# A hybrid mixer and mixture-of-experts layer: expert token lists made in DRAM, down products one item later

## The chip, the cores and the metric

The kernel runs on one core of one Trainium2 chip. Its time is the device time of one launch, in microseconds (us), and the median of three runs is 2895.78 us (2894.49 to 2897.89). All arithmetic of size is float32 on TensorE (PE). The other engines are VectorE (DVE), ScalarE (ACT), GpSimd (POOL) and SyncE (SP); SP issues nearly all plain DMAs, POOL the indirect ones.

## What is computed

One decoder layer over 1024 tokens of width 1024. Its first 60% (projections, three token mixers, gates) is untouched here. The rest is the output projection with the residual, a normalisation, and this mixture of experts:

```python
scores = sigmoid(h @ router_w)                    # 1024 x 64
# the best 4 of 8 groups, then the best 8 experts of each token; wts: their scores, normed, x 2.5
for e in 64 experts:                              # rt: the tokens that chose e
    hid = silu(h[rt] @ w1[e]) * (h[rt] @ w3[e])   # 1024 -> 256
    y[rt] += (hid @ w2[e]) * wts[rt, e]           # 256 -> 1024
y += (silu(h @ ws1) * (h @ ws3)) @ ws2            # the shared expert
x = x + g2 * y
```

## The kernel before

The 1024 tokens are eight tiles of 128. The routing stage is a loop over the tiles (PE's loop stands behind `shared_down`). For tile i PE does `out_proj(i)` (32 products of 128x512), `route(i-1)` (the normalised rows turned, then the router), and for tile i-2 the shared expert (`shared_up`, 16 products; `shared_down`, two transposes and 8 products) and `rank` (how many tokens before this one chose each expert). DVE does `residual`, `shared_hidden`, `choose` (the top-k), `slots` and `shared_out`. The rows h go to DRAM (`h2_d`, L439) and the residual with the shared expert to `y_d` (`store_shared`, L435), to which the experts' rows are added later by indirect DMAs.

The expert stage is a loop over items. An item is one expert and up to 256 of its tokens; an expert with more gets a further item behind the 64. There are 67 items here. They come in four sizes, which this text calls A (up to 64 tokens), B (65 to 128), C (129 to 192) and D (193 to 256). C and D have a second block of rows: 93 blocks in all, of which 63 are full and 30 are half ones, for which PE packs two 64-row products side by side (`up_half`, `down_half`). For item i (`pe_item`), PE does in this order: the up products of the first block (L1096 full, L1100 half); for C and D the transposes of the second block's rows (L1090), of the first hidden block (L1106) and the second up products; `turn_rows` for the next item (L1090, 8 transposes); the last hidden block's transposes (L1106 full, L1110 half); `token_lists` (L1084), which makes the list of item i+3 as 16 small products of one-hot matrices (`oh`, built by DVE at L1996 and L2000) with the table of token numbers and weights; and the down products (L1115 full, L1122 half). ACT copies turned rows and turned hidden blocks out of PSUM (L1467, L1473) and does the silu (L1470). DVE multiplies the hidden block (L2029), sums the list and makes the indices (L2022, L2026), weighs the outputs (L2033, or L2037 and L2039), and builds the one-hots for item i+4. POOL gathers rows of h (`fetch_first`, `fetch_second`, L608) for the items i+3 and i+2, waits until the earlier scatter has landed (`added.wait(e_sc)`), and scatters the weighed rows with an add into `y_d` (L612).

SP loads an item's three weight blocks of 1024 KB (L429, L430, L431) into one of four buffers once the item four before is done. The first two items' weights are asked for as soon as the last output projection is through. Each engine's order is written out by hand, with semaphores between the engines.

Between the two stages all token lists need the counts of all tiles: DVE writes the token columns and the item table, splits the table into three bfloat16 parts (L2049 to L2052), and three rounds of one-hot, list products and sum give the first three lists, one after the other.

Of the kernel before, what the change touches and what calls it, by code (L numbers as in the profile page):

```python
# [25 lines left out]
P = 128  # L26
# [8 lines left out]
def layer_kernel(nc, a, out):  # L35
# [23 lines left out]
    with ctx:  # L59
# [10 lines left out]
        y_d = dram("y_d", [T + P, D])  # L70

# [33 lines left out]
        def view(at, *shape):  # L105
# [6 lines left out]
            if len(shape) == 3:  # L112
# [50 lines left out]
        slotn = view(0, T)  # L163
# [12 lines left out]
        NX = NE + 4  # L176
        NI = NE + NE // 2
        selall = view(8192, NT, NE)
        posm = view(8704, NT, NX)
        tw = view(9248, NT, NX, 2)  # L180

# [5 lines left out]

        twb = view(5120, 3 * NT * NX).bitcast(BF16).rearrange("p (i e s z) -> p i e s z", e=NX, s=3, z=2)
        rest = view(6912, NT, NX, 2)
        xg = [[view(12288, D), view(13312, D)], [view(7168, D), view(9248, D)]]  # L190
        xgT = [view(14336 + 1024 * j, KD, P) for j in range(2)]
        oh = [view(16384 + 512 * j, T // 2).bitcast(BF16).rearrange("p (i n) -> p i n", n=P) for j in range(2)]
# [6 lines left out]
        lst = sb("lst", [P, 4, 2, 2])  # L199
        tab = sb("tab", [P, 3, NI + 8], I32)  # L200
        NV = NI + 8 - NE
        past, over, items = view(12000, NV)[0:NE, :], view(12040, 3)[0:NE, :], view(12048, 3, NV)[0:NE]
# [70 lines left out]
        e_w = [sem(f"e_w{b}") for b in range(2)]  # L273
        e_clear, e_go = sem("e_clear"), sem("e_go")
        s_tc, s_tp, s_ts, s_tv, s_to = (sem("s_t" + n) for n in "cpsvo")
# [5 lines left out]
        e_oh, e_lst, e_red, e_idx, e_oh1, e_lst1, e_idx1, e_sc, e_all, f_o = (  # L281
            sem("e_" + n) for n in ("oh", "lst", "red", "idx", "oh1", "lst1", "idx1", "sc", "all", "out"))
        e_w += [sem(f"e_w{b}") for b in (2, 3)]
        to_clear = [*e_xg[0], *e_xg[1], *e_Ta, *e_Tb, *e_xTa, *e_xTb, *e_H, *e_si, *e_hid, *e_hT, *e_hc, *e_O, *e_ob,
                    e_oh, e_lst, e_red, e_idx, e_oh1, e_lst1, e_idx1, e_sc, e_all, f_o, *e_w[2:]]
# [68 lines left out]
        def first_slot(eng, i):  # L354
            return eng.value_load(tab[0:1, 2, bass.ds(i, 1)], min_val=0, max_val=T - WIDE)

        I1 = NE - 4
        NC = T // P
# [4 lines left out]
        def _(sp):  # L363
# [63 lines left out]
            def load_expert(e, b):  # L427
# [3 lines left out]
                sp.dma_start(w2[b], one(a["exp_w2"]).rearrange("(k p) n -> p k n", p=P)).then_inc(e_w[b], 16)  # L431
# [11 lines left out]
            for b in range(2):  # L443
                load_expert(b, b)
            for i in range(NT - 3, NT):
                store_shared(i)
            sp.wait_ge(e_clear, 1)
            sp.wait_ge(s_sO, NT)
            sp.wait_ge(e_xg[0][0], 16)
            for b in range(2, 4):  # L450
                load_expert(b, b)
            with sp.Fori(1, I1 // 4) as it:
                for q in range(4):
                    sp.wait_ge(e_oh, 4 * it + q - 1)
                    load_expert(4 * it + q, q)
            with sp.Fori(I1 // 4, NI // 4) as it:
                with sp.If(tokens(sp, 4 * it) > 0):
                    for q in range(4):
                        with sp.If(tokens(sp, 4 * it + q) > 0):
                            sp.wait_ge(e_oh, 4 * it + q - 1)  # L460
                            load_expert(expert_of(sp, 4 * it + q, NE - 1), q)
# [10 lines left out]
        def _(pool):  # L472
# [104 lines left out]
            for n in range(48):  # L577
# [5 lines left out]
                g.dma_start(gt[n % 3], proj_d[row]).then_inc(s_g[n % 3], 16)  # L583
            pool.wait_ge(s_mg, 32)
# [7 lines left out]

# [8 lines left out]
            g.dma_start(y_d[T:T + P, :], xg[0][0]).then_inc(e_sc, 16)  # L602
            pool.wait_ge(s_so[0], 16 * (NT // 2))
# [27 lines left out]
            second, added = Count(pool, "second"), Count(pool, "added", 16, 16)  # L631
            for e in range(2):
                pool.wait_ge(e_idx1, e + 1)
                pool.sem_inc(e_go, 1)
                n = tokens(pool, e)
                fetch_first(n, e, e)
                fetch_second(n, e, e)
            pool.wait_ge(e_idx1, 3)
# [6 lines left out]
            def pool_item(it, q):  # L645
                i, p = 4 * it + q, q % 2
                n, n_2, n_3 = tokens(pool, i), tokens(pool, i + 2), tokens(pool, i + 3)
                now = pool.snap(i + 3)
# [4 lines left out]
                pool.wait_ge(e_ob[0], now)  # L653
# [19 lines left out]

            with pool.Fori(0, I1 // 4) as it:
                for q in range(4):
                    pool_item(it, q)
            with pool.Fori(I1 // 4, NI // 4) as it:
                with pool.If(tokens(pool, 4 * it) > 0):
                    for q in range(4):
                        with pool.If(tokens(pool, 4 * it + q) > 0):  # L680
                            pool_item(it, q)
# [7 lines left out]
        def _(pe):  # L689
# [316 lines left out]
            def route(i):  # L1006
                pe.wait_ge(s_h2, i + 1)
                if i >= 2:
                    pe.wait_ge(s_ya, i - 1)
# [49 lines left out]
            for i in range(NT + 2):  # L1059
                if i < NT:  # L1060
                    out_proj(i)
                if i >= 2:
                    shared_up(i - 2)
                if 1 <= i <= NT:
                    route(i - 1)
                if i >= 2:
                    shared_down(i - 2)
                    rank(i - 2)
# [5 lines left out]
            mm.then_inc(s_cn, 1)  # L1074
            pe.wait_ge(s_tp, 1)
            t.matmul(psum[0:NE, 7, 128:129], strict[0:NE, 0:NE], over[:, 0:1], start=True, stop=True).then_inc(s_ts, 1)
            pe.wait_ge(s_tv, 1)
# [1057 lines left out]
```

## Time and profile before

| | |
|---|---|
| median of 3 runs | 2895.78 us |
| the profiled execution | 2897.56 us, its span 2895.9 us |
| PE busy | 2730.2 us, 94% of the span |
| DVE, ACT, POOL busy | 39%, 20%, 12% |
| mean granted TensorE clock | 0.974 of 2.4 GHz |
| DMA | 442.26 MB, 153 GB/s over the span |
| routing stage, from the first output projection | 1525 to 1787 us |
| gap between the stages | 1787 to 1820 us |
| expert stage on PE | 1820 to 2868 us |

The shares are averages over stages with different limits. The expert stage and the gap ahead of it are 37% of the span, and the change touches these and the routing stage alone. A group's row gives the engine time of its instructions and the idle time of that engine just before them; a matmul's end is modelled, so what one costs in a dense stream is read as the distance between starts.

### The profile page before, as it was taken

Reading aid. Unit: us, or ns where it says so; the run is one execution under the profiler, and the core shown is the slowest. Engines: PE = TensorE matmul, PEld = TensorE weight load, DVE = VectorE, ACT = ScalarE, POOL = GpSimd, SP = SyncE. Lnnn points to the kernel's source line nnn. Section 1 sums busy time; section 2 is a strip of 40 time slices with the busy share of each in tenths; the row PEclk is TensorE's granted clock in tenths of the full one; section 3 lists DMA queues with packets and bytes.
Section 4 is the critical chain, followed back from the end, with each engine's and each line's share of the span. In section 5 each row is a group of like instructions: output and inputs, shape, how many; then the busy total and the mean of one; then the engine's idle time right before and its main releaser. Section 6 shows DMA issues by size and latency. Waiting matters only on the chain.

```text
span 2895.9 us, 32644 instructions
## 1 busy us (share of the span) xinstructions
PE 2730.2 (94%) x10465; PEld 1414.7 (49%) x10466; DVE 1141.2 (39%) x2772; ACT 584.0 (20%) x1037; POOL 343.9 (12%) x344
## 2 busy tenths in 40 slices
PE   5999999999999899999998997999999999999995
PEld 2444555555545355555444444444545545545543
DVE  3374333333246446554345656322223223323222
ACT  3211222222221222331111111111111111111110
POOL 0000000000110000000110000212222222222221
PEclk8999999999999999999999998999999999999998
DMA  7112323321432332222332103877779879979974
GB/s 271 30 29 84 87 73 95 99 90 51 137 81 62 87 80 73 77 88 80 106 114 86 44 37 131 284 229 228 254 223 307 283 245 312 321 227 338 326 243 94
DMA packets 125537, 442.26 MB, mean 153 GB/s; under 512 B 16252, under 2 KB 18404, under 8 KB 108224
## 3 DMA queue, kind: packets, MB, share of 16 engines
q1 hardware_dynamic: 86688, 311.10, 29.8%
q0 software_dynamic: 38752, 129.89, 17.9%
q8 instruction: 58, 0.95, 0.1%
q14 instruction: 39, 0.32, 0.0%
HBM read 371.95 MB, written 81.31 MB: 157 GB/s over the span
## 4 chain that ended last, share of the span: by engine, by line
PE 84%; DVE 6%; issue 5%; ACT 2%; SPq 1%; DMA 1%; DVEq 1%; POOL 0%; POOLq 0%; ACTq 0%
PE psum L740 27%; PE psum L1096 15%; PE psum L1115 8%; PE psum L981 6%; PE psum L1002 4%; PE psum L1100 3%; PE psum L1084 3%; PE psum L938 2%; PE psum L1122 2%; PE psum L833 2%; PE psum L815 2%; PE psum L1055 1%; PE psum L1090 1%; PE psum L824 1%; DVE work L2029 1%
## 5 line engine op out<-in xcount | busy, mean ns | idle before, releaser
L740 PE MATMUL psum<-hT,ring 128*128 128x512 f32 x1152 | 514.1, 599 | 9.5 <-ACT work L1302 8.8
L740 PE MATMUL psum<-ring,hT 128*128 128x512 f32 x896 | 402.7, 604 | 3.0 <-DVE hT L1596 3.0
L740 PEld LDWEIGHTS psum<-hT,ring 128*128 128x128 f32 x1152 | 215.5, 192 | 253.5 <-issue 242.2
L740 PEld LDWEIGHTS psum<-ring,hT 128*128 128x128 f32 x896 | 169.6, 194 | 199.3 <-issue 198.8
L1096 PE MATMUL psum<-hT,work 128*128 128x512 f32 x560 | 249.1, 598 | 0.0
L1470 ACT ACTIVATE work<-psum 128x256 f32<-128x256 f32 x93 | 35.7, 384 | 870.1 <-PE psum L1096 690.8
L1302 ACT ACTIVATE work<-psum 128x512 f32<-128x512 f32 x128 | 76.0, 595 | 636.3 <-PE psum L740 636.1
L2029 DVE TENSOR_TENSOR work<-work,psum 128x256 f32<-128x256 f32 x93 | 39.2, 422 | 403.5 <-ACT work L1470 399.2
L1096 PE MATMUL psum<-ring,work 128*128 128x512 f32 x448 | 197.9, 595 | 0.0
L612 POOL DMA_INDIRECT y_d<-work,put x93 | 148.7, 1599 | 246.9 <-issue 223.8
L608 POOL DMA_INDIRECT work<-h_d,idx x96 | 98.4, 1025 | 629.7 <-DVE idx L2026 373.7
L1096 PEld LDWEIGHTS psum<-hT,work 128*128 128x128 f32 x560 | 105.3, 191 | 134.9 <-issue 134.9
L981 PE MATMUL psum<-work,ring 128*128 128x512 f32 x384 | 165.0, 593 | 0.0
L2033 DVE SCALAR_TENSOR_TENSOR work<-psum,lst,work 128x1024 f32<-128x1024 f32 x63 | 80.9, 1284 | 182.1 <-PE psum L1115 182.1
L1096 PEld LDWEIGHTS psum<-ring,work 128*128 128x128 f32 x448 | 84.1, 190 | 107.6 <-issue 107.6
L1676 DVE CUSTOM_DVE_ANT_0 work<-psum,work 128x128 f32<-128x128 f32 (+6 forms) x56 | 38.7, 692 | 232.0 <-issue 218.4
L1115 PE MATMUL psum<-ring,work 128*128 128x512 f32 x280 | 126.6, 600 | 0.0
L1002 PE MATMUL psum<-ring,hT 128*128 128x512 f32 x256 | 114.5, 607 | 3.5 <-DVE work L1892 2.7
L981 PEld LDWEIGHTS psum<-work,ring 128*128 128x128 f32 x384 | 73.0, 190 | 91.3 <-issue 91.2
L1467 ACT ACTIVATE work<-psum 128x512 f32<-128x512 f32 x188 | 102.1, 595 | 45.5 <-PE psum L1090 42.2
L1084 PE MATMUL psum<-work 128*128 (+1 forms) x1120 | 87.9, 171 | 23.1 <-DVE work L1996 12.1
L1090 PEld LDWEIGHTS psum<-ident,work 128*128 128x128 f32 x752 | 86.2, 141 | 45.5 <-issue 45.5
(353 smaller groups left out, 3209.0 us busy)
## 6 DMA issues: line engine op xcount, KB each, us to landing
ring<-in_exp_w SPq DMA_DIRECT2D x100, 1024.0 KB, 10.9
hT<-in_exp_w SPq DMA_DIRECT2D x68, 1024.0 KB, 9.6
work<-in_exp_w SPq DMA_DIRECT2D x33, 1024.0 KB, 12.9
ring<-in_w_in SPq DMA_DIRECT2D x16, 2048.0 KB, 13.0
proj_d<-work SPq DMA_DIRECT2D x104, 256.0 KB, 2.0
work<-in_ada_w POOLq DMA_DIRECT2D x16, 1024.0 KB, 5.9
work<-proj_d POOLq DMA_DIRECT2D x56, 256.0 KB, 2.9
work<-proj_d POOLq DMA_DIRECT2D x20, 512.0 KB, 5.0
```

Of the source, the lines that this page charges most:

```text
L608: return g.indirect_dma_start(x[0:n], None, h2_d, bass.IndirectOffsetOnAxis(ap=i[0:n], axis=0), bounds_check=T - 1, oob_is_err=False)
L612: return g.indirect_dma_start(y_d, bass.IndirectOffsetOnAxis(ap=i[0:n], axis=0), x[0:n], None, bounds_check=T + P - 1, oob_is_err=True, co ...
L740: mm = t.matmul(bank(u % 3), l, r, start=(k == 0), stop=(k == KD - 1))
L981: mm = t.matmul(bank(n % 3), w[:, k, j * P:(j + 1) * P], yT[br][:, k, half * BW:(half + 1) * BW], start=(k == 0), stop=(k == 3))
L1002: mm = t.matmul(bank(half), hT[:, k, i * P:(i + 1) * P], slot(("wo", half))[:, k, :], start=(k == 0), stop=(k == KD - 1))
L1084: mm = t.matmul(psum[:, 2, 8 * j:8 * j + 6], oh[j][:, i, :], twb[:, i, bass.ds(e, 1), :, :].rearrange("p o s z -> p (o s z)"), start=(i == ...
L1090: mm = t.transpose(psum[:, k // 4, (k % 4) * P:(k % 4 + 1) * P], x[:, k * P:(k + 1) * P], ident[:, :])
L1096: return t.matmul(bank(3 + j), xgT[j][:, k, :], w13[b][:, :, k, :], start=(k == 0), stop=(k == KD - 1))
L1100: mm = t.matmul(psum[HALF * f:HALF * (f + 1), 3 + j, :].rearrange("p (w n) -> p w n", w=2)[:, :, 0:P], xgT[j][:, k, 0:HALF], w13[b][:, :, ...
L1115: mm = t.matmul(bank((6, 0)[j] + half), hidT[j][:, k * P:(k + 1) * P], w2[b][:, k, half * BW:(half + 1) * BW], start=(k == 0), stop=(k == ...
L1467: s.activation(xgT[j][:, 4 * half:4 * half + 4, :].rearrange("p k n -> p (k n)"), bank(half), ACT.Copy).then_inc((e_xTa, e_xTb)[half][j], 1)
L2033: v.scalar_tensor_tensor(out=ob[j][p], in0=banks(b, 2), scalar=lst[:, q, j, 1:2], in1=g2b, op0=ALU.mult, op1=ALU.mult).then_inc(e_ob[j], 1)
```

## The change

1. Routing also makes the lists. `choose` gives each token its eight experts' numbers in order (`cnt`, `eq8`) and their weights, `slots` computes for each of the eight a row of a DRAM table `list_d` (place in the expert's list, then expert), and POOL scatters them: eight indirect DMAs of 128 rows of 8 bytes (token, weight) per tile, 64 in all (`list_tokens`). The table is filled with padding first. Behind the last tile POOL reads the whole table back into SBUF (`lists`, 512 KB), and its first 64 places once more into the other half of the partitions (`lists2`). A list is then two columns of SBUF.
2. `token_lists`, the one-hots, the bfloat16 split and the sums are gone. DVE copies three small slices per item instead (`take_list`).
3. In the expert loop PE does the down products of item i-1 (`downs`) behind the first up products and the row transposes of item i. DVE weighs and POOL scatters one item later too, and POOL's gathers wait for PE's `e_Tb` as well. The few items behind the 64 keep item order (`pe_item_alone`).
4. The up weights have a semaphore of their own, apart from the down weights; those of item i are asked for when the up products of item i-4 are through, the down weights later.
5. In the routing stage the shared expert and its store lag three tiles, not two, `rank` comes right behind `out_proj`, `slots` moves into `residual`. The counting and the item table are laid between the last shared blocks. SP asks for the weights of items 0 and 1 behind the store of tile 4, for those of item 2 when the last shared block is done, and issues the store of tile 7 behind these.

```diff
+            def list_tokens(i):
+                pool.wait_ge(s_dst, i + 1)
+                if i == 0:
+                    pool.wait_ge(s_ls, 16)
+                for k in range(TOPK):
+                    g.indirect_dma_start(list_d, bass.IndirectOffsetOnAxis(ap=dest[:, i, k:k + 1], axis=0), pay[:, i, k, :], None,
+                                         bounds_check=P * NE * NT - 1, oob_is_err=True).then_inc(s_ls, 16)
...
+            list_tokens(6)
+            list_tokens(7)
+            pool.wait_ge(s_ls, 16 + 16 * NT * TOPK)
+            rows = list_d.rearrange("(p r) c -> p r c", p=P)
+            g.dma_start(lists, rows).then_inc(s_ls, 16)
...
+            store_shared(NT - 2)
+            sp.wait_ge(s_sO, NT)
             sp.wait_ge(e_clear, 1)
-            sp.wait_ge(s_sO, NT)
-            sp.wait_ge(e_xg[0][0], 16)
+            load_up(2, 2)
+            load_down(2, 2)
+            store_shared(NT - 1)
+            load_up(3, 3)
...
+                    i = 4 * it + q
+                    sp.wait_ge(e_Tb[0], i - 2)
+                    load_up(i, q)
+                    sp.wait_ge(e_hT[0], i - 2)
+                    load_down(i - 1, (q + 3) % 4)
...
+                    fetch_ahead(it, q)
+                    with pool.If(pool.snap(n_last) > 0):
+                        add_rows(pool.snap(n_last), 1 - q % 2, pool.snap(4 * it + q + 2))
...
+            for i in range(NT + 1):
                 if i < NT:
                     out_proj(i)
                 if i >= 2:
+                    rank(i - 2)
+                if i >= 3:
+                    shared_up(i - 3)
+                if i >= 1:
+                    route(i - 1)
+                if i >= 3:
+                    shared_down(i - 3)
+            shared_up(NT - 2)
+            rank(NT - 1)
...
-                pe.wait_ge(e_oh, now)
-                pe.wait_ge(e_idx, now)
-                token_lists(listed).then_inc(e_lst, 1)
...
+                up_first(it, q, n)
+                pe.reg_mov(n_now, tokens(pe, 4 * it + q + 1))
                 with pe.If(n > P):
+                    turn_second(p)
+                with pe.Else():
+                    turn_next(it, q)
+                with pe.If(pe.snap(n_last) > 0):
+                    downs(pe.snap(n_last), (q + 3) % 4, 16 * (it + 1) if q else 16 * it, pe.snap(4 * it + q + 1))
+                pe.nop()
+                pe.reg_mov(n_last, n)
+                with pe.If(n > HALF):
                     pe.wait_ge(e_hid[0], now)
                     turn_hidden(0)
+                    with pe.If(n > P):
+                        up_second(q, n)
+                        turn_next(it, q)
+                        turn_hidden_second(n)
...
+                link(v.tensor_tensor_scan(out=cnt, data0=ones[:, 0:NE], data1=picked, initial=0.0, op0=ALU.mult, op1=ALU.add))
+                link(v.tensor_tensor(cnt, cnt, picked, ALU.mult))
+                link(v.tensor_tensor(eq8, wide(cnt), col_i[:, 1:TOPK + 1].unsqueeze(2).to_broadcast([P, TOPK, NE]), ALU.is_equal))
+                link(v.tensor_tensor(of8, eq8, wide(sel), ALU.mult))
+                link(v.tensor_reduce(flat8, of8, AX.X, ALU.add))
...
+                link(v.tensor_tensor(of8, eq8, at8.unsqueeze(1).to_broadcast([P, TOPK, NE]), ALU.mult))
+                link(v.tensor_reduce(sum8, of8, AX.X, ALU.add))
...
+            table()
+            dve.wait_ge(s_ls, 16 + 16 * NT * TOPK + 16)
...
+            shared_out(NT - 1)
```

## Rows read from the trace of the kernel before

**Rows 1.** Stretches: busy time of PE, PEld, DVE, ACT, POOL, clock, DMA share, GB/s.

```profile
1742.00:1820.00 78.00, 50.09 (x258) 30.66 (x257) 49.82 (x157) 13.04 (x19) 4.72 (x5) 0.82 0.37 137
1820.00:2870.00 1050.00, 1033.36 (x4684) 531.07 (x4684) 302.57 (x508) 163.18 (x373) 243.40 (x186) 1.00 0.81 265
2418.00:2490.00 72.00, 71.50 (x411) 39.74 (x411) 26.68 (x48) 12.22 (x28) 19.41 (x15) 1.00 1.01 360
```

**Rows 2.** Groups, 1820 to 2870 us: count, busy us, mean ns, idle before.

```profile
L608 POOL DMA_INDIRECT work<-h_d,idx x94 | 96.1, 1023 | 564.2 <-DVE idx L2026 373.7 <-issue 190.5
L1084 PE MATMUL psum<-work 128*128 x1072 | 86.2, 171 | 7.6 <-issue 5.6
...
L2080 DVE COPY put<-idx 128x2 int32<-128x2 int32 x67 | 10.9, 163 | 0.0
L1110 PE MATMUL psum<-ident,work 128*128 128x128 f32 x30 | 9.8, 326 | 2.5 <-DVE work L2029 2.5
```

**Rows 3.** PE's timeline of a B item: start, length, then the instructions.

```profile
1939.30 0.44 PE L1106 MATMUL psum<-ident,work 128*128 128x128 f32 x2
1939.76 1.30 PE L1084 MATMUL psum<-work 128*128 x16
1940.97 3.67 PE L1115 MATMUL psum<-work 128*128 128x512 f32 x8
```

**Rows 4.** The same at the end of a D, an A and a C item.

```profile
1897.37 0.44 PE L1106 MATMUL psum<-ident,work 128*128 128x128 f32 x2
1898.15 1.28 PE L1084 MATMUL psum<-work 128*128 x16 [0.34 <-issue]
1899.35 7.11 PE L1115 MATMUL psum<-ring,work 128*128 128x512 f32 x16
...
2452.49 1.28 PE L1084 MATMUL psum<-work 128*128 x16
2453.81 1.94 PE L1122 MATMUL psum<-work 128*64 128x512 f32 x8
...
2715.27 0.33 PE L1110 MATMUL psum<-ident,work 128*128 128x128 f32 x1
2715.73 1.27 PE L1084 MATMUL psum<-work 128*128 x16
2716.90 3.67 PE L1115 MATMUL psum<-ring,work 128*128 128x512 f32 x8
```

**Rows 5.** POOL's timeline: scatters of a B item (first), then of A items.

```profile
2450.48 1.58 POOL L612 DMA_INDIRECT y_d<-work,put  x1 [3.82 <-DMA y_d<-work,put]
...
2462.26 1.46 POOL L612 DMA_INDIRECT y_d<-work,put  x1 [5.98 <-issue]
...
2651.17 1.44 POOL L612 DMA_INDIRECT y_d<-work,put  x1 [5.85 <-issue]
...
2660.52 1.56 POOL L612 DMA_INDIRECT y_d<-work,put  x1 [3.32 <-issue]
```

**Rows 6.** Issue to landing: of L435's stores, of L431's down weights, of L612's scatters.

```profile
DMA to landing us min/median/max: 2.6/3.7/12.4
...
DMA to landing us min/median/max: 10.4/12.9/24.6
...
DMA to landing us min/median/max: 4.8/8.3/12.8
```

**Rows 7.** The chain that ended last: start, length, instructions, around the stages' border.

```profile
1687.73 6.26 PE psum L1055 x8
...
1726.89 13.80 PE psum L1002 x32
...
1752.75 3.70 PE psum L1055 x8
...
1819.87 8.45 PE psum L1096 x16
```

**Rows 8.** A DVE operation over 512 columns: busy us, mean ns.

```profile
L1941 DVE TENSOR_TENSOR work<-work 128x512 f32<-128x512 f32 x6 | 4.2, 692 | 0.2
```

More of the change, by code:

```diff
@@ new lines, in turn_second, with turn_next, turn_hidden_second @@
+            def turn_second(p):
+                fetched[p].up()
+                fetched[p].wait(e_xg[1][p])
+                turn_rows(1, xg[1][p])
+            def turn_next(it, q):
+                pe.wait_ge(e_xg[0][1 - q % 2], 32 * it + 16 * ((q + 1) // 2) + 16)
+                turn_rows(0, xg[0][1 - q % 2])
+            def turn_hidden_second(n):
+                with pe.If(n > P + HALF):
+                    second.wait(e_hid[1])
+                    turn_hidden(1)
+                with pe.Else():
+                    second.wait(e_hid[1])
+                    turn_half_hidden(1)
+                pe.nop()
@@ new lines, in downs @@
+            def downs(n, q, weights, turned):
+                with pe.If(n > HALF):
+                    with pe.If(n > P):
+                        with pe.If(n > P + HALF):
+                            second.wait(e_hc[1])
+                            pe.wait_ge(e_v[q], weights)
+                            down(1, q)
+                        with pe.Else():
+                            second.wait(e_hc[1])
+                            pe.wait_ge(e_v[q], weights)
+                            down_half(1, q)
+                        pe.nop()
+                    pe.nop()
+                    pe.wait_ge(e_hc[0], turned)
+                    pe.wait_ge(e_ob[0], turned)
+                    pe.wait_ge(e_v[q], weights)
+                    down(0, q)
+                with pe.Else():
+                    pe.wait_ge(e_hc[0], turned)
+                    pe.wait_ge(e_ob[0], turned)
+                    pe.wait_ge(e_v[q], weights)
+                    down_half(0, q)
+                pe.nop()
@@ L1879, in _ @@
             dve.wait_ge(s_rw, 32)
+            link(v.tensor_scalar(col8, col_i[:, 0:NE], float(NT), None, ALU.mult))
+            for i in range(NT):
+                ins = v.tensor_scalar(pay[:, i, :, 0:1].rearrange("p k o -> p (k o)"), tok[:, i:i + 1].to_broadcast([P, TOPK]), float(FAR), None, ALU.add)
+            link(ins)
+            dve.wait_ge(s_ls, 16)
             def residual(i):
@@ L1953, in _, with table @@
+            def table():
+                dve.wait_ge(s_ts, 2)
+                made = psum[:, 7, 256:256 + 3 * NV].rearrange("p (a b) -> p a b", a=3)
+                link(v.tensor_copy(tab[:, 0, NE:NE + NV], made[:, 0, :]))
+                link(v.tensor_scalar(tab[:, 1, NE:NE + NV], made[:, 1, :], float(NE), None, ALU.add))
+                v.tensor_copy(tab[:, 2, NE:NE + NV], made[:, 2, :]).then_inc(s_tab, 1)
+            for i in range(NT + 1):
                 if i < NT:
                     residual(i)
-                if i >= 2:
-                    shared_hidden(i - 2)
@@ new lines, in _ @@
+                if i >= 1:
+                    choose(i - 1)
+                if i >= 3:
+                    shared_out(i - 3)
+            slots(NT - 1)
+            shared_hidden(NT - 2)
+            count_items()
+            shared_out(NT - 2)
+            list_items()
+            shared_hidden(NT - 1)
+            table()
+            dve.wait_ge(s_ls, 16 + 16 * NT * TOPK + 16)
+            some = lambda x, e, n, c: x[:, bass.ds(e, n), c:c + 1].rearrange("p j o -> p (j o)")
+            three = lambda x, c: x.rearrange("p (e j) c -> p e j c", j=NT)[:, 0:3, 0:2, c:c + 1].rearrange("p e j o -> p e (j o)")
@@ L2060, in _, with hidden_second @@
+            dve.reg_mov(n_last, 0)
+            dve.wait_ge(s_ls, 16 + 16 * NT * TOPK + 32)
+            link(v.tensor_copy(lst[:, 0:3, :], three(lists, 1)))
+            link(v.tensor_copy(lst2[HALF:P, 0:3, :], three(lists2[HALF:P], 1)))
             dve.wait_ge(s_ys[0], 16 * (NT // 2))
             dve.wait_ge(s_ys[1], 16 * (NT // 2))
[L2063 to L2078 removed]
+            def hidden_second():
+                second.up()
+                second.wait(e_si[1])
+                hidden(1)
```

480 lines of the change are left out of this document (229 added, 251 removed).

## The prediction

> **What bounds the kernel now.** I read the page's slices first (PE nine tenths busy in nearly all of them), then the windows, which give each engine's busy time by stage. In the expert stage PE is busy 1033 of 1050 us at a granted clock of 1.00 (its upper level, 2.4 GHz), DVE 303, ACT 163, POOL 243 us, and DMA has a share of 0.81 [rows 1]. So PE's stream of products is the bound there, and what leaves that stream comes off the time, until something else is late. In the stretch around the gap between the stages PE is busy 50 of 78 us, at a mean clock of 0.82 [rows 1]: dependencies bound it. The profiled execution took 2897.56 us (span 2895.9, 1.7 outside it). I make the sum against it; the median of the runs is 1.8 lower, so the result is lowered by 1.8.
>
> **The list products leave PE.** They are 1072 products in 67 lists [rows 2], one per item (the copy L2080 runs once per item, x67). Their busy time of 86 us is made of overlapping modelled ends, so I price a list by starts. From the list's first product to the down products it is 1.21 us in a B item [rows 3], 1.20 in D, 1.32 in A, 1.17 in C [rows 4]. PE's timeline has 17 A, 24 B, 13 C and 13 D items (its C items are those where a full block is followed by a half one; A and C together are the 30 half blocks [rows 2]). 17 x 1.32 + 24 x 1.21 + 13 x 1.17 + 13 x 1.20 = 82.3 us.
>
> Ahead of the list there is a gap too. A transpose stands 0.14 us from the next (8 of them and the 2 of the hidden block take 1.36), so in B the list starts 0.19 us later than it could (0.46 - 0.27 [rows 3]), in C 0.31 (0.46 - 0.15) and in D 0.51 (0.78 - 0.27) [rows 4]. In B nothing is late behind the hidden transposes any more, since their wait has the down products of the previous item (3.5 us) as cover, so I count 24 x 0.19 = 4.6 us. In C and D the second hidden transposes still come right behind their wait for DVE, and the next item's products come behind them with more branches than now; I take that this gap stays (0), its other bound is 13 x 0.31 + 13 x 0.51 = 10.7 us. Together 86.9 us, bounds 82 to 98.
>
> **The down products one item later.** Between hidden transposes and down products lie ACT's copy and two semaphores. The list hides them now. In the loop the next item's up products (3.6 or 6.9 us) hide them, so the deferral costs nothing and keeps the gain whole. It doesn't for the last item of the loop and the three behind it: about 1 us each is open there (copy 0.4, two hops), 4 us, bounds 0 to 6. The next rows' copies by ACT now have only 0.3 us of transposes as cover in C and D. The first half of them is enough to start the up products, and is ready about 1.3 us behind the start of 1.04 us of transposes: nothing, within the gap above.
>
> **What is late next in the loop: scatters.** A scatter is issued when the one before has landed. In a run of A items they follow each other by 9.35 us, while PE needs 8.0 per item; behind a B item by 11.8 us, PE now 13.2 [rows 5]. After the change PE needs 6.6 for A and 11.8 for B. DVE has two output buffers, so it may be one item behind before PE stops. Two stretches are nearly all A and B. Items 35 to 41 (A A B A A B B): scatters 4 x 9.35 + 3 x 11.8 = 73 us, PE 62 after the change (72 now [rows 1]). Items 50 to 55 (B A B A A A): 61 against 50. The excess of 11 us in each, less the slack of about one item (6 to 9 us), leaves 2 to 5 us in each, and the gathers, which POOL issues in the same order and which cost 1.02 us of POOL and up to some 9 us to land, may add as much. I take 10 us in all, bounds 0 and 25 (all the excess and a little at the single A items). DVE's three small copies per item and its register loads take the place of 1.2 to 2.4 us of one-hots and cost nothing.
>
> **The weights.** The A and B stretch ran at 360 GB/s with a share of 1.01 [rows 1], so DMA is full there already. An A item moves 3.15 MB of weights and 0.5 of rows. What saves it is depth: set beside the landings of the loads (L429 and L430), the up products started 9 us behind their weights at the least (item 56), 13 to 20 in that stretch. The new order asks for the up weights when the up products of item i-4 end, 3 to 8 us sooner than now, and PE runs away by 4 to 5 us over the lead of three items. Nothing, then, and the rival below prices the opposite.
>
> **Routing stage.** PE's work is the same. Before the last output projection ends there is one shared tile less (up 6.9, down 3.7 to 6.3 with its clock, waits 1: 12 us sooner) and behind it one more. In the first tiles without shared work DVE becomes late by about 4 us, since a tile gives PE only 19 us there while `choose` and `slots` grow. Both get some 3.4 and 1.6 us longer (three and one passes over 512 columns at 0.69 [rows 8], and small ones). Later a tile lasts 32 us on PE against 27 on DVE, so that costs nothing. The last output projection ended at 1726.89 + 13.80 = 1740.7 [rows 7]; it will end about 8 us sooner, at 1733. Call that moment 0. PE: rank, up, route and down until 17; rank(6) waits for `choose(6)` until 20; up, route, down until 37; up, rank(7) until 46; `slots(7)`, counts until 50; down 55; up 62; table 63; last down ends at 68. DVE's `shared_out` ends at 71.
>
> The lists: `slots(7)` ends at 49. Eight scatters on POOL at 1.3 us (a gather takes 1.02 [rows 2], 0.3 between two; an adding scatter 1.6, so the other bound is 1.9): 59 to 64. Landing 2, read-back of 512 KB 4: 65 to 70. First gather issued at 68 to 72, landed at 72 to 76. So the lists are no later than the shared expert by much.
>
> The store of tile 7 is the late one. ACT copies no rows until all stores to `y_d` have landed, and SP issues that store behind 3 MB of weights for item 2, asked for at 68. A store issued in such a place before, behind the loads of items 0 and 1, took 12.4 us instead of 3.7, and landed with the last of them; weights alone take 12.9 to land [rows 6]. So: 68 + 13 + 1.5 = 83, ACT's copy 0.7, first up products at 84, that is 1733 + 84 = 1817 against 1819.9 [rows 7]. Gain 3 us. Bounds: 13 us better, if the store overtakes, and with tile 3 not late 17; 5 us worse, if the small writes are slow. By the Trainium skill (DMA: Bandwidth & Descriptors, Queues, rings and completion order) descriptors of one queue are consumed in ring order on each DMA engine, which agrees with that 12.4 us. The same page (Specifications) has transfers under 512 B do a read-modify-write; no row shows an 8-byte scatter.
>
> **Sum.** 86.9 - 4 - 10 + 3 = 76 us. 2897.56 - 76 - 1.8 = 2819.8; I say 2820. The ends: 98 + 17 = 115 gives 2781, and 82 - 6 - 25 - 5 = 46 gives 2850.
>
> **Rivals.**
> 1. The start is early as well (the store isn't held back, no tile late) and the scatters keep up: 87 to 93 + 13 to 17, less 4: about 2795. For it: the loop's slack. Against it: 12.4 us [rows 6]. Chance 0.17.
> 2. DMA binds in the loop. Where its share is about 1 (some 290 us in 2150 to 2280, 2410 to 2510 and 2620 to 2720 us), the stretch can't get shorter, and 10 to 13% of it is lost: 30 us more, 2850. For it: 360 GB/s at 1.01 [rows 1]. Against it: 10 us windows in the same stretches reach 400, and the lead of 9 us. The Trainium skill speaks for it: DMA: Bandwidth & Descriptors (Specifications) has an HBM limit of about 358 GB/s per core, by which that stretch is at its end already; the short windows disagree. Chance 0.15.
> 3. Slower than before: the clock. Waits of a few tenths to 1 us ahead of eight down products of the shared expert left them at 6.26 us (largely at the lower level, 1.2 GHz) where they take 3.70 at the upper [rows 7]. If new waits in the expert loop did this, each would cost 2.6 us; the gain of 76 is gone from 30 of 67 items, and with all it is 2994. Against it: item 62 waits 1.2 us now and pays nothing. Chance 0.03.
> 4. The lists come much later than the shared expert. If a small scatter took POOL 8 us, the last eight alone cost 64 us, and the 64 of them would fill the routing stage: 2890 or more. Nothing in the rows is near it. Chance 0.03, half of it slower.
>
> The forecast has 0.62. What a measurement can tell from no change is 0.2%, 6 us. Range 2785 to 2850. Faster 0.94, same 0.02, slower 0.04.
>
> **What would show it.** PE busy falls by 80 to 90 us, and no L1084 group is there. Right: up to down in C and D with the gap unchanged; waits of PE in runs of A items for POOL's gathers or DVE's outputs, 10 us in all; first up products near 1817 with ACT waiting for the store's landing. Wrong: waits for weights at the up products (rival 2), a clock under 1.00 in the loop (rival 3), the last gather released by the read-back (rival 4), first up products before 1808 (rival 1).

## The result and the profile after

The changed kernel takes 2823.79 us (median of 4 runs, 2820.7 to 2826.04), the kernel before beside it 2896.84 us; the ratio is 0.9743, 95% interval 0.9723 to 0.9764. The forecast was 2820. The profiled execution took 2825.91 us, 71.7 less than that of before.

The groups of PE in the expert loop (count, busy us, mean ns, idle before). No group of list products is there [rows 2], and the wait for gathered rows is new:

```profile
L1144 PE MATMUL psum<-hT,work 128*128 128x512 f32 x560 | 249.0, 598 | 19.0 <-ACT work L1557 14.9 <-issue 4.1
...
L1138 PE MATMUL psum<-ident,work 128*128 128x128 f32 x744 | 98.3, 275 | 13.2 <-DMA work<-h_d,idx 13.2
```

The windows (busy time of PE, PEld, DVE, ACT, POOL, clock, DMA share, GB/s) from the last output projection to the first up products, of the loop, and of a run of A and B items; they answer to [rows 1]:

```profile
1731.90:1825.40 93.50, 66.33 (x238) 37.24 (x236) 51.37 (x156) 13.82 (x21) 32.21 (x32) 0.85 0.48 175
1825.00:2795.00 970.00, 938.60 (x3612) 462.29 (x3612) 205.81 (x482) 170.04 (x374) 235.89 (x185) 1.00 0.84 282
2585.00:2635.00 50.00, 42.04 (x233) 21.01 (x233) 13.14 (x36) 9.26 (x20) 14.95 (x13) 0.97 1.03 366
```

PE's timeline of a B item (start, length, instructions), against [rows 3]:

```profile
1936.65 7.03 PE L1144 MATMUL psum<-ring,work 128*128 128x512 f32 x16
1943.52 1.04 PE L1138 MATMUL psum<-ident,work 128*128 128x128 f32 x8
1944.40 3.60 PE L1165 MATMUL psum<-work 128*128 128x512 f32 x8
1947.83 0.38 PE L1154 MATMUL psum<-ident,work 128*128 128x128 f32 x2
1948.05 2.31 PE L1144 MATMUL psum<-hT,work 128*128 128x512 f32 x5
```

An undisturbed B item lasts 11.40 us (1948.05 - 1936.65) where it was 13.14; A went from 8.0 to 6.66, C from 20.07 to 18.89, D from 25.1 to 23.75.

The same timeline on the way to the loop shows a wait, up products of 9.30 us and down products of 5.06 at a lower clock, and the wait for ACT; in the chain that ended last the landing of a store fills that wait:

```profile
1752.91 2.52 PE L1076 MATMUL psum<-work,ones 128*128 128x64 f32 x12 [4.26 <-DVEq L2027]
...
1755.65 9.30 PE L1087 MATMUL psum<-ring,work 128*128 128x512 f32 x16
...
1788.06 5.06 PE L1104 MATMUL psum<-work 128*128 128x512 f32 x8 [0.47 <-ACT work L1553]
...
1802.23 3.70 PE L1104 MATMUL psum<-work 128*128 128x512 f32 x8 [0.47 <-ACT work L1553]
1811.51 1.94 PE L1138 MATMUL psum<-ident,work 128*128 128x128 f32 x8 [5.58 <-issue]
1825.44 5.14 PE L1144 MATMUL psum<-hT,work 128*128 128x512 f32 x8 [11.99 <-ACT work L1557]
```

```profile
1808.86 15.20 DMA y_d<-work
1825.44 8.59 PE psum L1144 x16
```

Where the 71.8 us of span went (2895.9 - 2824.1), cut at the same instructions in both traces, in us:

| stretch | before | after | difference |
|---|---|---|---|
| up to the first output projection (untouched) | 1524.9 | 1521.0 | -3.9 |
| to the end of the last one | 215.9 | 210.9 | -5.0 |
| to the first up products | 79.1 | 93.6 | +14.5 |
| to the end of the last down products | 1048.7 | 969.6 | -79.1 |
| to the end | 27.4 | 29.1 | +1.7 |

So the loop gave more than the whole gain, and the way to it took 9.5 us back. The 3.9 us of the untouched part are close to the spread of single executions: in the nine profiled runs of the changed kernel and its variants the first output projection starts between 1518.6 and 1525.7 us, in the three of the kernel before and its variants between 1524.9 and 1530.3.

### The profile page after: what moved, and what is told of

Read it like the earlier page. It is cut to its first block, busy times and chain, and to the rows that moved or that the text cites. A ratio compares the mean times of both kernels' runs of the same rounds, so it can differ in the third digit from the quotient of the medians.

```text
span 2824.1 us, 30914 instructions
## 1 busy us (share of the span) xinstructions
PE 2645.7 (94%) x9345; PEld 1349.7 (48%) x9346; DVE 1065.9 (38%) x2799; ACT 588.0 (21%) x1035; POOL 416.6 (15%) x413
## 4 chain that ended last, share of the span: by engine, by line
PE 76%; DMA 9%; issue 6%; DVE 5%; ACT 2%; SPq 1%; POOLq 0%; POOL 0%; DVEq 0%; ACTq 0%
PE psum L789 28%; PE psum L1144 12%; PE psum L1165 6%; DMA y_d<-work,put 6%; PE psum L1030 6%; PE psum L1051 4%; PE psum L987 2%; PE psum L1148 2%; PE psum L882 2%; PE psum L864 2%; PE psum L1138 2%; PE psum L1172 1%; PE psum L1104 1%; PE psum L873 1%; PE psum L1087 1%
## 5 line engine op out<-in xcount | busy, mean ns | idle before, releaser
L647 POOL DMA_INDIRECT y_d<-work,put x93 | 142.7, 1534 | 192.1 <-issue 132.4
L1138 PE MATMUL psum<-ident,work 128*128 128x128 f32 x752 | 100.2, 277 | 18.8 <-DMA work<-h_d,idx 13.2
```

The lines of the kernel that those rows point to most:

```text
L647: return g.indirect_dma_start(y_d, bass.IndirectOffsetOnAxis(ap=i[0:n], axis=0), x[0:n], None, bounds_check=T + P - 1, oob_is_err=True, co ...
L1138: mm = t.transpose(psum[:, k // 4, (k % 4) * P:(k % 4 + 1) * P], x[:, k * P:(k + 1) * P], ident[:, :])
```

## Experiments

Three questions: what each part of the change is worth in the loop, what makes the gathers late, and what holds the start. The changed kernel again, the deferral undone, the lists doubled and the store first ran on one chip, the rank products moved and the store first once more on another, the other four on a third, each beside the kernel before.

**The changed kernel again.** 

> The changed kernel again, beside the other kernels of this set on one chip, so that each can be set against it. Expected 2824 us, 72 us under the kernel before; the first up products start at about 1825 us and the loop of items up to the end of the last down products takes about 970 us. Both theories below expect the same of it.

Measured: 2822.71 us (2819.14 to 2826.24), ratio 0.9741 (0.9725 to 0.9757), loop 969.5 us. So the kernels of the different chips can be set side by side within some us.

**The deferral undone.** PE calls `pe_item_alone` in all items, DVE and POOL follow:

```diff
-                    pe_item(it, q)
-            downs(pe.snap(n_last), 3, 16 * (NE // 4), NE + 1)
+                    pe_item_alone(it, q)
```

> The changed kernel with the deferral undone: each item's down products stand behind its own hidden transposes, as in the kernel before, and VectorE and the queue of scatters follow the same order; lists still come from DRAM and the lag of the shared expert stays at three tiles. Theory one (deferral hides a round trip of hidden copy and weights of an item): every one of the 67 items pays about 0.5 to 1 us between the last transposes and its down products, where before the list products stood, so 35 to 65 us are given back: 2860 to 2890. Rival (the list products' removal alone carries the gain and other work covered the trip): within 10 us of the changed kernel, 2815 to 2835.

Measured: 2861.6 us, ratio 0.9874 (0.9857 to 0.989), 39 us over the changed kernel; loop 1006.6 us. Theory one holds. PE's waits in its loop (us in total, times, longest), and a B item of its timeline:

```profile
PE psum L1168 <- ACT work L1558: 25.5, 30, 0.9
PE psum L1161 <- ACT work L1558: 22.1, 37, 0.6
```

```profile
1940.19 0.44 PE L1150 MATMUL psum<-ident,work 128*128 128x128 f32 x2
1941.22 3.69 PE L1161 MATMUL psum<-work 128*128 128x512 f32 x8 [0.60 <-ACT work L1558]
```

All 67 items now wait for ACT's hidden copy, 47.6 us together. From the hidden transposes to the down products it is 1.03 us, and with the list between them it was 1.67 [rows 3]. So taking the list away without the deferral frees 42 of the loop's 79 us (1048.7 to 1006.6) and the deferral frees the other 37. These 37 are net: PE waits for no gathered row here, while the changed kernel, being faster, has 13.2 us of such waits. The half of a list's time that lay over that copy would have been lost.

**The lists doubled in the kernel before.**

```diff
+                token_lists(listed)
                 token_lists(listed).then_inc(e_lst, 1)
```

> The kernel before with the 16 list products of each item issued twice, the second set over the first, so that nothing else changes. Theory one (they stood on the path that sets the end, at full price): 17 x 1.32 + 24 x 1.21 + 13 x 1.17 + 13 x 1.20 = 82 us more, 2970 to 2985. Rival (part of their time lay over the wait for the hidden copy that the down products have anyway): clearly less, 20 to 60 us more; then the gain of the change came in part from the deferral.

Measured: 2940.95 us, ratio 1.0146 (1.0127 to 1.0166), 43 us over before. The number is the rival's, but the reason is another. A B item and the end of a D item:

```profile
1951.70 1.68 PE L1084 MATMUL psum<-work 128*128 x32
1953.24 3.68 PE L1115 MATMUL psum<-work 128*128 128x512 f32 x8
```

```profile
1933.10 1.68 PE L1084 MATMUL psum<-work 128*128 x32 [0.25 <-issue]
1934.64 8.81 PE L1115 MATMUL psum<-ring,work 128*128 128x512 f32 x16
```

32 products take 1.54 us to the next start where 16 took 1.21: the second list costs 0.33 us, 22 us in 67 items.
**A second list for another item.** The extra list was to have register instructions of its own, so it is made for another item:

```diff
                 listed = expert(i + 3)
+                other = expert(i + 2)
...
+                token_lists(other)
                 token_lists(listed).then_inc(e_lst, 1)
```

> The kernel before with two sets of list products per item, the extra set for another item so that it has register instructions of its own for the addresses of its tables; its result is overwritten by the real set. When the same set was issued twice (e3_lists_twice), the copy cost 43 us in all and no 82: there the first 8 of the 16 products started 124 ns apart, each behind a register instruction in the queue of weight loads, and the 8 others and the 16 of the copy 25 ns apart. Theory one (a list costs what its address instructions cost, eight times 0.1 us, and it stands on the path in full): 77 to 90 us over the kernel before, 2975 to 2988. Rival (a second set costs 0.33 to 0.6 us whatever its addresses, since part of a list lies over the wait for ACT's copy of the hidden rows): 35 to 50 us more, about 2941.

Measured: 2994.27 us, ratio 1.0345 (1.0314 to 1.0376), 97 us over before. The total is over theory one's range, and most of it is not the list. The extra list has its own register instructions in 22 of the 67 items only. There the trace has 16 register instructions for the 32 products (the first count below, 2000 to 2003 us); in the other 45 it has 8, as with the repeated list (the second, 1958 to 1960.5 us):

```profile
L1084 PEldq FUSED_REGOPS  x16: 46/46/74, 2000.3 to 2002.4; - x16
L1084 PEldq FUSED_REGOPS  x8: 46/46/74, 1958.8 to 1959.7; - x8
```

```profile
2000.47 2.41 PE L1084 MATMUL psum<-work 128*128 x32 [0.35 <-issue]
2002.79 7.11 PE L1115 MATMUL psum<-ring,work 128*128 128x512 f32 x16
```

By the single records, the time from the first list product to the products behind the list is 2.30 us (median) in the 22 items, 1.46 in the 45, and 1.20 in the kernel before. So a second list costs 1.10 us with its address instructions, near theory one's price, and 0.26 without. An undisturbed B item, one of the 45, is only 0.1 to 0.3 us longer than before. Together the lists make some 36 us (22 x 1.10 + 45 x 0.26) of the 92 by which this loop is longer (1140.8 against 1048.7). The rest stands elsewhere: PE's timeline at the turn of the loop, PE's waits in the loop, and the queue that loads instructions (transfers, MB, share):

```profile
1886.16 3.67 PE L1115 MATMUL psum<-work 128*128 128x512 f32 x8
1894.61 5.67 PE L1096 MATMUL psum<-hT,work 128*128 128x512 f32 x7 [4.77 <-issue]
```

```profile
PE psum L1096 <- issue: 15.7, 5, 4.9
PE psum L1100 <- issue: 5.6, 2, 4.8
```

```profile
q8 instruction: 94, 1.54, 0.6%
```

PE stood up to 4.9 us for nothing that the trace shows, four times for 4.7 to 4.9 us at the first up products of items 4, 8, 20 and 32 (the loop's body holds four items), and 94 transfers loaded instructions in this loop where the kernel before had 11 and the changed one 7. The D items 4 and 32, behind such a stop, took 30.5 and 30.6 us where one without a stop took 25.2. PE's idle time in the loop is 27 us more than in the kernel before. The added products alone don't bring this: the doubled list adds as many, and that loop has 13 transfers and no such stop. What this kernel has beyond those are the further register instructions and loads. That its longer code is fetched again at the turn is likely, but not shown.

**Few weights.** In the loop, from item 4 on, SP loads only a small part of each item's weights; the kernel leaves the rest out, and its output is another one:

```diff
-                    load_up(i, q)
+                    part_up(i, q)
...
-                    load_down(i - 1, (q + 3) % 4)
+                    part_down(i - 1, (q + 3) % 4)
```

> The changed kernel, but in the loop of 64 items SyncE loads only an eighth of the up weights and a quarter of the down weights of each item from item 4 on, so most products run on weights left there by earlier items and the output is another one: this kernel leaves that work out. Every instruction of PE, DVE, ACT and POOL stays. Theory one (the load on the DMA engines makes gathers land late, which PE's waits for gathered rows in the changed kernel, 13.2 us in 8 waits, come from): gathers land in 4 to 6 us where their median was 8.9, the waits for them fall to 0 to 4 us, and the time is 9 to 15 us under the changed kernel, 2808 to 2815. Rival one (POOL's order, gather behind a scatter that waits for the landing before it, makes them late by itself): the waits stay above 8 us and the time within 5 us of the changed kernel. Rival two (weights bound the loop as well): the loop falls by more than 15 us below 969.

Measured: 2808.64 us, ratio 0.9692 (0.9675 to 0.9709), loop 951.6 us. Windows of its loop and of the same kind of stretch in the kernel with the early store (below), then the issue to landing of its gathers:

```profile
1830.00:2780.00 950.00, 933.67 (x3611) 461.56 (x3610) 203.68 (x482) 169.24 (x372) 235.59 (x185) 1.00 0.51 121
```

```profile
1830.00:2780.00 950.00, 922.18 (x3566) 456.27 (x3564) 204.18 (x474) 167.40 (x368) 233.21 (x182) 1.00 0.85 284
```

```profile
DMA to landing us min/median/max: 2.9/4.6/13.1
```

With the share at 0.51 gathers land in 4.6 us (9.0 in the changed kernel), PE waits for none, and the loop is 18 us shorter. That is over the 15 us that I had set as the mark of rival two. Still, I read it as the gather waits (13.2 us) and some lower clock behind them, not as a bound of the weights: PE has no wait for weights at up or down products in either kernel.

**Scatters that write and don't add.** The addition is left out, so the output is another one here too:

```diff
-                                            bounds_check=T + P - 1, oob_is_err=True, compute_op=ALU.add)
+                                            bounds_check=T + P - 1, oob_is_err=True)
```

> The changed kernel, but the scatters of an item's rows to the output write instead of adding, so each row holds only the last contribution: the addition in DRAM is left out. Theory (an adding scatter takes POOL longer to issue, 1.6 us, and DRAM longer to finish, so the chain of scatters in runs of small items holds the gathers): landings of scatters fall from a median of 10.1 us to 6 to 8, the gather waits of PE from 13 to under 8 us, the time by 4 to 8 us to about 2818. Rival (the landing is set by the load of the DMA engines, not by the addition): landings within 1 us of the changed kernel's, time within 4 us of 2823.

Measured: 2805.54 us, ratio 0.9686 (0.967 to 0.9702), loop 953.5 us. Gather waits of PE, and a scatter's issue to landing here and in the changed kernel:

```profile
PE psum L1138 <- DMA work<-h_d,idx: 1.8, 2, 1.0
```

```profile
DMA to landing us min/median/max: 3.3/8.6/13.3
```

```profile
DMA to landing us min/median/max: 4.8/10.1/15.1
```

Landings fell by only 1.5 us and POOL's issue from 1.53 to 1.0, and still 11 of the 13 us of waits went, with DMA at a share of 0.75 for the same weights. The time fell by 17 us where theory had 4 to 8. The gathers still landed in 8.4 us (9.0 in the changed kernel), so it is mostly their issue that came earlier; this run also takes some load off DMA, so it does not part the two cleanly. With few weights the order is kept and the waits are gone; here most of the load is kept and they are nearly gone. So I take neither load nor order alone as the cause, but the chain of both, which POOL's timeline of the changed kernel shows, with PE's wait behind it:

```profile
2592.84 1.55 POOL L647 DMA_INDIRECT y_d<-work,put  x1 [4.95 <-DMA y_d<-work,put]
2596.31 1.00 POOL L643 DMA_INDIRECT work<-h_d,idx  x1 [1.93 <-issue]
```

```profile
2605.33 1.09 PE L1138 MATMUL psum<-ident,work 128*128 128x128 f32 x8 [3.02 <-DMA work<-h_d,idx]
```

The scatter stands 4.95 us for the landing before it, the gather of item i+3 is behind it in POOL's order, and PE waited 3.02 us for that gather at 2605.3. A few us off either link nearly end it.

**The store of tile 7 first.**

```diff
+            store_shared(NT - 1)
             load_up(2, 2)
             load_down(2, 2)
-            store_shared(NT - 1)
```

> The changed kernel with one thing turned round: SyncE issues the store of tile 7's output ahead of the loads of item 2's weights and not behind them. Theory one: in the changed kernel the start of the loop hangs on the landing of that store, 15.2 us after its issue behind 3 MB of weights in the same queue, where the other stores of this line landed in 2.6 us. ScalarE then waits 22.5 us for it, and the first up products start at 1825.4. With the store in front they start when rows are turned and copied, at 1813 to 1815, and the time falls by 10 to 12 us to about 2813. Rival: something else is ready only just before (the gathered rows, the weights of item 0), or item 2's weights now come late and the first items wait for them: the time stays at 2822 to 2826.

Measured: 2810.27 us (2807.25 to 2814.09), ratio 0.9697 (0.968 to 0.9713), 12.4 us under the changed kernel on the same chip. Its chain that ended last:

```profile
1807.99 3.92 DMA y_d<-work
1813.28 9.02 PE psum L1144 x16
```

Theory one holds: the store lands in 3.9 us, the first up products start at 1813.3, and the loop is the same length (968.9), so item 2's weights are not missed. This version beats both kernels; its later run, beside the moved rank products below, gave 2815.35 us, ratio 0.9719 (0.9696 to 0.9742), so its lead over the changed kernel is 7 to 12 us.

**A lag of two tiles, with the store first.** The shared expert goes back to tile i-2 in PE's, ACT's and DVE's loops:

```diff
-                if i >= 3:
-                    shared_up(i - 3)
+                    shared_up(i - 2)
```

> The kernel with the store of tile 7 ahead of item 2's weights (e1_store_first, 2810), and the shared expert lags two tiles behind again and not three. Theory one (the lag of three gives the output projections, and with them the lists, some 5 us of lead, and takes them back as a third shared tile behind the last output projection at a slow clock): the last output projection ends 8 to 12 us later, the tail behind it is 10 to 14 us shorter, and the time is within 6 us of 2810. Rival (with a lag of two, the lists now bind the start, since routing of tile 7 ends later and only two shared tiles stand over it): the first up products wait for the first gathered rows and the time is 8 to 15 us more, 2818 to 2825.

Measured: 2822.57 us, ratio 0.9742 (0.9724 to 0.9759), 12 us over the first run of the version with a lag of three and 7 over its later one (2815.35). The last output projection ends at 1740.8 (1731.9 in the changed kernel), as theory one has it, but the rest is the rival's:

```profile
1807.74 0.78 PE L1130 MATMUL psum<-work,ones 64*128 64x120 f32 x2 [5.42 <-DVE work L2088]
1823.80 1.97 PE L1135 MATMUL psum<-ident,work 128*128 128x128 f32 x8 [15.28 <-DMA work<-h_d,idx]
```

PE has no shared tile left and waits 15.3 us for the first gathered rows. The read-back of the lists, asked for at 1805.85, now runs beside item 2's weights, asked for from 1805.5; the first gather is issued 10.8 us behind it, and 6.9 in the changed kernel, and lands in 7.1 us where it took 4.4 with the store first and a lag of three. The first up products start at 1825.7, 12 us later than with a lag of three. So that lag is worth 7 to 12 us, but only because the lists need that lead.

**The rank products behind the up products,** in the last turn of the loop, with the store first; beside it the kernel with the store first again.

```diff
-                if i >= 2:
+                if 2 <= i < NT:
                     rank(i - 2)
                 if i >= 3:
                     shared_up(i - 3)
+                if i == NT:
+                    rank(i - 2)
```

> The kernel with the store of tile 7 ahead of item 2's weights (e1_store_first, 2810), and in the last turn of the routing loop the rank products of tile 6 stand behind the shared up products of tile 5 and not ahead of them. Theory one: in the changed kernel PE stood 4.26 us at these rank products, waiting for VectorE's choice of tile 6, and the up products behind them then took 9.22 us where the others took 7.08 (clock). With the up products in front of the wait they cover it and keep the clock: PE's stream from there is 6 to 8 us earlier, routing of tile 7 and the lists with it, the first up products start at 1805 to 1807, and the time is 2802 to 2805. Rival (something that the routing of tile 7 doesn't carry binds the start: the gathered rows, or VectorE, which gets the ranks of tile 6 later by 5 us and does its slots ahead of the hidden rows of tile 5): the time stays at 2808 to 2812.

> The kernel e1_store_first once more, on the same chip as e10_rank_behind, so that the two are set against each other with few us between them. Both theories expect 2808 to 2812, 13 us under the changed kernel, with PE's wait of 4.26 us at the rank products of tile 6 and up products of 9.2 us behind it.

Measured: 2813.73 us, ratio 0.971 (0.9694 to 0.9727), against 2815.35 and 0.9719. No difference clear of noise; my theory fell. PE's timeline, and the windows of this kernel and of the first run with the early store:

```profile
1748.19 7.03 PE L1087 MATMUL psum<-ring,work 128*128 128x512 f32 x16
...
1759.09 1.32 PE L1060 MATMUL psum<-ident,work 128*128 128x128 f32 x8 [2.36 <-DVE work L2055]
1761.52 3.67 PE L1067 MATMUL psum<-work 128*128 128x64 f32 x16 [1.11 <-ACT work L1534]
...
1766.09 5.62 PE L1104 MATMUL psum<-work 128*128 128x512 f32 x8 [0.47 <-ACT work L1555]
```

```profile
1740.00:1816.00 76.00, 62.24 (x212) 34.33 (x211) 44.22 (x133) 11.57 (x18) 30.34 (x30) 0.83 0.48 178
```

```profile
1740.00:1816.00 76.00, 60.01 (x206) 33.64 (x207) 43.20 (x133) 11.39 (x17) 29.48 (x30) 0.87 0.48 174
```

The up products are early and at the full clock, as hoped. But the row transposes then wait 2.36 us for DVE's `shared_out` of the tile before, and behind the two waits the router products take 3.67 us and the next two sets of down products 5.62 and 6.50; with the rank products in front they took 2.00, 3.70 and 4.95. The wait moved, the lower clock moved with it, and the first up products start at 1812.4, against 1812.0 and 1813.3.

## Why the prediction was right, step by step

The measured time lies 4 us from the forecast, and that closeness is luck: the terms are off by up to 12 us each, in both directions (the sum, below). What was right is the mechanism in the loop.

**List products and gaps (86.9 us, bounds 82 to 98): right, 10 us short.** The undisturbed items give 24 x 1.74 + 17 x 1.34 + 13 x 1.18 + 13 x 1.35 = 97 us, and with few weights the loop is 97.1 us shorter than before. A and C came as priced (1.32, 1.17), D 0.15 us over its 1.20, and the C and D gap stayed, as I took (0.3 to 0.4 us ahead of the next up products). The mis-sized term is B: 1.74 for 1.40. From the rows' transposes to what follows them it is 0.88 us where it was 1.10 (1939.30 - 1938.20), the hidden transposes cost 0.22 and not 0.27, and the down products 3.43 and not 3.51.

**Deferral (-4 us): right.** The last four items wait for the hidden copy for 3.1 us (1.7 and 1.4), and it costs nothing else. What the prediction did not say in numbers is that it carries half of the 82 us: without it 47.6 us of waits stand where the lists stood (the deferral undone).

**Scatters and gathers (-10 us, bounds 0 to 25): right in place and size,** 13.2 us of waits in 8 places, seven of them in items 38 to 56. With few weights or plain scatters they vanish, and the loop gets 18 and 16 us shorter: the clock behind a wait adds some us (0.97 in 2585 to 2635 us).

**Weights (0) and rival 2: no wait for weights in the loop.** The stretch at a share of 1.03 and 366 GB/s lost its time at gathers and at the clock behind them. Rival 2 took a full DMA for a bound on the weights, where it was a longer landing of the gathers. The Trainium skill (DMA: Bandwidth & Descriptors, Specifications) has an HBM limit of about 358 GB/s per core. This trace does not agree: that stretch ran at 366, above it, and the loop as a whole went from 265 to 282 GB/s.

**Routing and start (+3 us, bounds -5 to +17): wrong in size, and outside its lower bound.** First up products were to come at 1817 and came at 1825.4; with the 3.9 us by which the untouched part was shorter, the miss is 12 us. 3 us of it lie ahead of the last output projection's end, where the tiles gave 5.0 us and not 8. The others, from that end on (1731.9, 1733 expected): the last shared down products end 74 us behind it and not 68, since up products took 9.30 us and down products 5.06 where the sum had 7.0 and 3.7, with 1 us more at the rank wait and the rest in shorter pieces. I had the lower clock behind waits in [rows 7] and used it for rival 3 alone, not for the stretch in which new waits were certain. Then the store: asked for behind the weights, as forecast, it landed 18.1 us after the first of these was asked for (1805.96), where 14.5 were counted. The mechanism was right (ring order within the queue, as the page cited in the prediction has it), and the early store gives its price: first up products 12 us sooner (1813.3), and 7 to 12 us of the time. The lists were no later than the shared expert: the first gather was issued 72 us behind that end (68 to 72 counted) and landed at 76. The small scatters took POOL 0.97 us and 0.30 between two, 1.27 each for 1.3:

```profile
1794.44 0.98 POOL L613 DMA_INDIRECT list_d<-work  x1 [0.30 <-issue]
...
1803.74 1.07 POOL L643 DMA_INDIRECT work<-h_d,idx  x1 [6.31 <-issue]
```

**The sum** of 76 us against 71.7 missed by little because errors cancelled: the loop gave 6 us more (10 in the lists, 1 in the deferral, less 3 in the gathers and 2 in the clock), the start 12.5 less, and the untouched part 3.9 more and the end 1.7 less, neither of which was in it. Rival 1 is one moved line away in its first half: with the store first 2810 to 2815, and the gather waits are most of what is left to its 2795. Rivals 3 and 4 did not come.

## What to carry to other kernels

Work that stands between a step and the engine that waits for its result hides that result's trip: before pricing its removal, read what comes due behind it, and move independent work (here the next item's up products) into its place. A small transfer on which the next stage hangs must not be issued behind megabytes in the same queue, even where these are wanted early too. A wait of two to four us ahead of TensorE products can cost more than itself, and moving the wait moves that cost; and a wait for a gather is often POOL's order, one transfer's landing holding the issue of the next.

## What the runs showed of the hardware that I had not expected

- Small products whose weights have an address from a register start 124 ns apart, and 25 ns apart when the address is used again (the lists doubled). A list of 16 costs 1.10 us in the first case and 0.26 in the second (the second list for another item).
- A loop body with a second list for another item had PE standing up to 4.9 us at its turn, with 94 instruction transfers where there were 11. The same 16 products more per item without the further address instructions had 13 and no such stop.
- POOL's small scatters are slower beside wide DVE operations; no run took one of them away. In six tiles, the two scatters that began while DVE's two operations over 128x1024 ran took 1.74 to 2.48 us each, and the other 52 of the 64 at most 1.08. Below are two of the twelve, beside operations from 1739.50 to 1743.65. The DVE operations took 2.0 to 2.1 us each also in the first two tiles, which had no scatter beside them. In one other place DVE may be the slowed one: its operation over 128x64 took 1.44 us (0.25 a tile later, in the run with the early store) as POOL's memset began. The Trainium skill (GPSIMD Engine Reference, Specifications) names DVE operations with two SBUF inputs as contending with POOL, which is the form of those over 128x1024:

```profile
1740.17 2.29 POOL L613 DMA_INDIRECT list_d<-work  x1 [0.30 <-issue]
1742.77 1.75 POOL L613 DMA_INDIRECT list_d<-work  x1 [0.31 <-issue]
...
1749.62 1.97 POOL L631 MEMSET work<- 128x1024 f32 x2
```

```profile
1749.20 1.44 DVE L2000 TENSOR_SCALAR work<-work 128x64 f32<-128x64 f32 x1
```
